# The front of a hybrid decoder layer: attention tiles set into the feature blocks of the input projection, with a ring of three banks

## What is computed

```python
xn = rmsnorm(x, n1)
h, cg, bg, q, k, v, r, a_lr, u, vv, ga, gb, gc = split_cols(xn @ w_in)
conv = sum(cp[:, i:i + t] * conv_w[i] for i in range(3))     # cp = past rows, then cg * h
y_a = (bg * conv) @ proj_a
log_a = log_sigmoid(a_lr @ gla_a2 + gla_a_b) / 16
# gated linear attention, 4 heads (dk 128, dv 256), chunks of 64 tokens
b = cumsum(log_a)                                            # within the chunk
att = where(mask, (q * exp(b)) @ (k * exp(-b)).T, 0)
o_i = att @ v_i + (q * exp(b)) @ s
s = exp(b_last) * s + (k * exp(b_last - b)).T @ v_i
o = rmsnorm(o, gla_ng) * silu(r);  y_b = o @ proj_b
# chunk mixing: chunks of 128 tokens, 4 groups
s = tril(ws) @ rmsnorm(gelu(vv), cm_ng) + bias;  y_c = (gelu(u) * s) @ proj_c
x = x + (sigmoid(ga) * y_a + sigmoid(gb) * y_b + sigmoid(gc) * y_c) @ w_out
x = x + hier_moe(rmsnorm(x, n2));  y = rmsnorm(x, final_g)
```

## Time and profile before

| | us |
|---|---|
| three runs | 2210.21, 2214.68, 2214.86 |
| median | 2214.68 |
| the profiled execution | 2213.19 |
| its span, from the first to the last instruction | 2211.5 |
| TensorE busy in the span | 1819.8 (82%) |
| VectorE, ScalarE, GpSimd busy | 552.6, 458.0, 187.4 |
| bytes moved by DMA | 419 MB, 190 GB/s on average |

### The profile page before, as it was taken

How to read it: one execution, slowest core, us unless ns; L and a number is a source line. 1 busy time by engine, 2 the same in 40 slices (tenths; PEclk the granted TensorE clock), 3 DMA queues, 4 the chain that set the end, 5 groups by cost and what they waited for, 6 DMA issues and landing times. The chain is left out here.

```text
span 2211.5 us, 24670 instructions
## 1 busy us (share of the span) xinstructions
PE 1819.8 (82%) x10166; PEld 1437.6 (65%) x10166; DVE 552.6 (25%) x733; ACT 458.0 (21%) x728; POOL 187.4 (8%) x214
## 2 busy tenths in 40 slices
PE   6999999999999999747765899799329787888770
PEld 6999999999999999624333899688313232333220
DVE  4100100003232200055554543332511001001006
ACT  5122211112211211143443200122001100100112
POOL 0000000000000000111110000000041111111100
PEclk9999999999999999866567999899669999999995
DMA  4222222322366552233313534443659999999976
GB/s 148 98 79 79 94 93 89 133 78 79 113 174 162 130 91 58 103 100 122 122 42 126 206 119 161 143 169 143 279 185 391 421 421 421 421 420 419 417 295 242
DMA packets 176373, 419.37 MB, mean 190 GB/s; under 512 B 38256, under 2 KB 116784, under 8 KB 150624
## 3 DMA queue, kind: packets, MB, share of 16 engines
q1 hardware_dynamic: 153056, 349.00, 44.2%
q0 software_dynamic: 23088, 69.14, 8.2%
q10 hardware_dynamic: 144, 0.03, 0.0%
HBM read 347.53 MB, written 86.33 MB: 196 GB/s over the span
## 5 line engine op out<-in xcount | busy, mean ns | idle before, releaser
L1939 PE MATMUL ps<-W,XT 128*64 128x512 f32 x512 | 257.9, 663 | 83.3 <-DMA W<-in_exp_w_dram 82.0
L1696 PE MATMUL ps<-XH,WH 128*128 128x384 f32 (+1 forms) x1176 | 263.4, 332 | 11.7 <-issue 7.8
L1696 PE MATMUL ps<-XL,WH 128*128 128x384 f32 (+1 forms) x1176 | 260.7, 330 | 0.0
L1696 PE MATMUL ps<-XH,WL 128*128 128x384 f32 (+1 forms) x1176 | 260.2, 329 | 0.0
L1940 PE MATMUL ps<-W,XT 128*64 128x512 f32 x512 | 258.4, 663 | 0.0
L1215 DVE TENSOR_TENSOR WL<-RAW,WH 128x2048 fp32r<-128x2048 f32 x34 | 77.9, 2293 | 631.9 <-ACT WH L928 610.7
L1939 PEld LDWEIGHTS ps<-W,XT 128*64 128x64 f32 x512 | 75.0, 152 | 231.2 <-issue 228.9
L1696 PEld LDWEIGHTS ps<-XH,WH 128*128 128x128 f32 x1176 | 201.4, 189 | 17.3 <-issue 13.5
L1659 PE MATMUL ps<-WH,XH 128*128 128x256 f32 x720 | 206.7, 287 | 5.2 <-ACT OT L936 2.0
L1660 PE MATMUL ps<-WL,XH 128*128 128x256 f32 x720 | 205.2, 285 | 0.0
L1661 PE MATMUL ps<-WH,XL 128*128 128x256 f32 x720 | 205.1, 285 | 0.0
(11 more groups left out here) (284 smaller groups left out, 2320.4 us busy)
## 6 DMA issues: line engine op xcount, KB each, us to landing
W<-in_exp_w_dram SPq DMA_DIRECT2D x192, 1024.0 KB, 25.2
RAW<-in_w_in_dram SPq DMA_DIRECT2D x34, 1024.0 KB, 5.3
feat<-OF POOLq DMA_DIRECT2D x24, 1088.0 KB, 4.4
sg<-feat SPq DMA_DIRECT2D x24, 544.0 KB, 5.5
tokd<-OT POOLq DMA_DIRECT2D x10, 1024.0 KB, 4.7
cbuf<-feat SPq DMA_DIRECT2D x16, 544.0 KB, 5.6
X<-in_x_prompt_dram SPq DMA_DIRECT2D x16, 512.0 KB, 4.4
W<-y SPq DMA_DIRECT2D x8, 1024.0 KB, 7.6
```

Of the source, the lines that this page charges most:

```text
L1696: last = pe.matmul(ps[:, 3 * f + g, 0:tn], w[:, k, :], x[:, k, t0:t0 + tn], start=(k == 0 and i == 0), stop=(k == nk - 1 and i == 2))
L1939: pe.matmul(ps[0:BR, 2 + s, :], XT[s][:, k, 0:BR], pair_of(u, k, DE), start=(k == 0), stop=(k == KD - 1))
```

## The change

The front and the attention stage become one stage; all else stays, but for the barriers' numbers and the places of two buffers. The token chunks are 512 columns wide: five of them (`T_COLS`), vv first, whose nine tiles stay in SBUF (vvt), 24 products with 512 columns for a tile. The sample tile takes the last 128 tokens in place of 64 and padding. The features are blocks of 128 columns, 49 `JOBS` in an order worked out in Python: low-rank, q and k of head 0, the four u, and then one block for each attention step J from -2 to 36, in which the conv features, the gates and the q and k of the next head stand; three gates are left at the end. A block's 72 products are three runs of 24 (`f_product`), one for each token group. All products of the front, the decay's (D), the mixing's (M) and the sample update's (SU) take banks 0 to 2 in turn (`RING`); before a bank is taken the emptying of the one three places before is waited for (`bank_free`, `EMPTIED`), on ScalarE, or on VectorE for cg, bg, M and SU. The attention has bank 3 for its output, bank 4 for both transposes, 5 and 6 for the updates, 7 for the scores.

In block n with step J, TensorE makes the key transpose of tile J + 2 and the scores of J + 1, the first run, the update of J + 1, the second run, the output of J and the transposes of J - 1, the third run, and what `extras` adds. h, cg, bg, u, q and k are no longer stored to DRAM: conv and mixing work on the bank and on SBUF. v and r still go through DRAM and come back tile by tile into five buffers each. The sample states are updated in place, two samples for each bank. The products with the decays are all on VectorE. The squares of vv are ScalarE's, one activation for each tile and group (`v_squares`), 36 in all. The loops of the front are written out.

```diff
+        def front_jobs():
+
+            others = [("H", 0)]
+            for c in range(NCH):
+                if c:
+                    others.append(("H", c))
+                others += [("CG", c), ("G", 3 * c), ("BG", c), ("G", 3 * c + 1), ("G", 3 * c + 2)]
+            others += [("G", g) for g in range(3 * NCH, 3 * KD)]
+            others = iter(others)
+            jobs = [("A", 0, None), ("Q", 0, None), ("K", 0, None)] + [("U", c, None) for c in range(NCH)]
+            for J in range(-2, STEPS + 1):
+                h, j = divmod(J, NT)
+                if 0 <= h < HEADS - 1 and j < 2:
+                    jobs.append(("QK"[j], h + 1, J))
+                else:
+                    jobs.append((*next(others), J))
+            return jobs + [(kind, c, None) for kind, c in others]
+        JOBS = front_jobs()
...
+        def extras(n):
+
+            kind, c, J = JOBS[n]
+            out = []
+            if (kind, c) == ("Q", 0):
+                out += [("D", 0, g) for g in range(3)]
+            if kind == "K" and c:
+                out += [("D", c, g) for g in range(3)]
+            if kind == "U":
+                out += [("M", c, g) for g in range(3)]
+            if J is not None and J > 0 and J % NT == 0:
+                out += [("SU", J // NT - 1, i) for i in range(DEC_B // 2)]
+            return out
...
+        def ring_jobs():
+            out = []
+            for i in range(len(T_COLS)):
+                for t in range(NT):
+                    out.append(("T", i, t))
+                    if (i, t) == (1, 0):
+                        out += [("WS", 0, 0), ("WS", 1, 0)]
+            for n, (kind, c, J) in enumerate(JOBS):
+                out += [(kind, c, g) for g in range(3)] + extras(n)
+            return out
+        RING = ring_jobs()
+        AT = {name: r for r, name in enumerate(RING)}
+        ON_DVE = ("CG", "BG", "M", "SU")
+        EMPTIED, n_of = [], [0, 0]
+        for name in RING:
+            e = int(name[0] in ON_DVE)
+            n_of[e] += 1
+            EMPTIED.append((e, n_of[e]))
...
+            def v_squares(t):
+                if t % 4 == 0:
+                    act.drain()
+                for g in range(NCH):
+                    act.activation(OFA[:, (t % 4 * NCH + g) * P:(t % 4 * NCH + g + 1) * P], vvt[:, t, g * P:(g + 1) * P], ACT.Square, accum_out=vss[:, t * NCH + g:t * NCH + g + 1])
...
+            tw_high(1)
+            t_empty(0, NT - 1)
+            for t in range(NT):
+                v_squares(t)
+            act.drain()
             act.activation(vrs[:], vss[:], ACT.Sqrt, bias=epsc[:], scale=1.0 / P).then_inc(cm_rt, 1)
...
+            for i in range(1, len(T_COLS)):
+                for t in range(NT):
+                    if t == 4 and 1 < i + 1 < len(T_COLS):
+                        tw_high(i + 1)
+                    t_empty(i, t)
...
+            def fw_high(n):
+                act.wait_ge(fw_in[n % 3], n // 3 * 16 + 16)
+                if n >= 2:
+                    act.wait_ge(ring_mm, job_done(n - 2))
+                act.activation(FHI[n % 2][:], FRAW[n % 3], ACT.Copy).then_inc(fw_hi, 1)
...
+            fw_high(0)
+            for n, (kind, c, J) in enumerate(JOBS):
+                if n + 1 < NJ:
+                    fw_high(n + 1)
+                if J is not None and is_tile(J + 2):
+                    k_copy(J + 2)
+                f_empty(kind, c, 0)
+                f_empty(kind, c, 1)
+                if is_tile(J):
+                    out_rms(J)
+                if J is not None and is_tile(J - 1):
+                    out_copy(J - 1)
+                f_empty(kind, c, 2)
+                if n in PREP:
+                    for g in range(3):
+                        decay_logits(PREP[n], g)
+                    decay_log(PREP[n])
+                if n - 2 in PREP:
+                    decay_exp(PREP[n - 2])
+            barrier(act, 1)
...
+            fw_low(0)
+            dve.wait_ge(g_c, 1)
+            for n, (kind, c, J) in enumerate(JOBS):
+                if n + 1 < NJ:
+                    fw_low(n + 1)
+                if J is not None and is_tile(J + 1):
+                    mask(J + 1)
+                if is_tile(J) and J % NT == 0:
+                    sample_queries(J // NT)
+                if is_tile(J) and J % NT == NFULL - 1:
+                    sample_keys(J // NT)
+                f_empty(kind, c, 0)
+                if J is not None and is_tile(J + 1) and (J + 1) % NT < NFULL:
+                    states(J + 1)
+                f_empty(kind, c, 1)
+                if is_tile(J):
+                    out_norm(J)
+                f_empty(kind, c, 2)
+                for what, h, i in extras(n):
+                    if what == "M":
+                        mix_empty(h, i)
+                    if what == "SU":
+                        sample_states(h, i)
+                if n - 1 in PREP:
+                    decay_sums(PREP[n - 1])
+                if n - 3 in PREP:
+                    decayed(PREP[n - 3])
...
+            def bank_free(*name):
+
+                r = AT[name]
+                if r >= 3:
+                    e, count = EMPTIED[r - 3]
+                    pe.wait_ge(ev[e], count)
+                return r % 3
 
...
-            def t_product(all_, tile):
-
-                s = all_.s
-                if not (all_.first and s * NT + tile < 3):
-                    pe.wait_ge(t_ev, all_.n * NT + tile - 2)
-                cols = slice(tile * P, tile * P + P)
+            def t_product(i, t):
+                s, b, cols = i % 2, bank_free("T", i, t), xcols(t)
                 for k in range(KD):
-                    last = three(ps[:, tile % 3, 0:CW], XH[:, k, cols], XL[:, k, cols], WH[s][:, k, :], WL[s][:, k, :],
-                                 k == 0, k == KD - 1)
-                last.then_inc(t_mm, 1)
-
-            def t_chunk(col, st, all_, here):
-                pe.wait_ge(wl_ready, all_.n + 1)
-                for tile in range(NT):
-                    t_product(all_, tile)
-                pe.drain().then_inc(w_used, 1)
+                    if t == 0 and k % 2 == 0:
+                        pe.wait_ge(tw_lo, 4 * i + k // 2 + 1)
+                    last = three(ps[:, b, :], XH[:, k, cols], XL[:, k, cols], THI[s][:, k, :], TLO[s][:, k, :], k == 0, k == KD - 1)
+                last.then_inc(ring_mm, 1)
...
+            def f_product(n, g):
+                kind, c, _ = JOBS[n]
+                b, to, tn = bank_free(kind, c, g), cols_of(g), TG[g][1]
+                if g == 0:
+                    pe.wait_ge(fw_lo, n + 1)
+                for k in range(KD):
+                    hi, lo = FHI[n % 2][:, k, :], FLO[n % 3][:, k, :]
+                    pe.matmul(ps[:, b, 0:tn], hi, XH[:, k, to], start=(k == 0), stop=False)
+                    pe.matmul(ps[:, b, 0:tn], hi, XL[:, k, to], start=False, stop=False)
+                    last = pe.matmul(ps[:, b, 0:tn], lo, XH[:, k, to], start=False, stop=(k == KD - 1))
+                last.then_inc(ring_mm, 1)
...
+            for n, (kind, c, J) in enumerate(JOBS):
+                if J is not None and is_tile(J + 2):
+                    k_transpose(J + 2)
+                if J is not None and is_tile(J + 1):
+                    scores(J + 1)
+                f_product(n, 0)
+                if J is not None and is_tile(J + 1) and (J + 1) % NT < NFULL:
+                    update(J + 1)
+                f_product(n, 1)
+                if is_tile(J):
+                    out_product(J)
+                if J is not None and is_tile(J - 1):
+                    out_transpose(J - 1)
+                f_product(n, 2)
+                for what, h, i in extras(n):
+                    if what == "D":
+                        decay_product(h, i)
+                    elif what == "M":
+                        mix_product(h, i)
+                    else:
+                        sample_update(h, i)
+            barrier(pe, 1)
...
-            def f_chunk(col, st, all_, here):
-                s = st.s
-                pe.wait_ge(wl_ready, all_.n + 1)
-                for f in range(2):
-                    if here.first and here.s == 0:
-                        pe.wait_ge(t_ev, NTC * NT)
-                    else:
-                        pe.wait_ge(f_ev, here.n * 2 + (f - 1))
-                    last = feature(f, WH[s][:, :, f * P:(f + 1) * P], WL[s][:, :, f * P:(f + 1) * P], KD, XH, XL)
-                    last.then_inc(f_mm, 1)
-                pe.drain().then_inc(w_used, 1)
```

More of the change, by code:

```diff
@@ L466, in tok, with bank, head_tile, is_tile @@
+        def bank(*name):
+            return AT[name] % 3
+        def head_tile(J):
+            return J // NT, J % NT
+        def is_tile(J):
+            return J is not None and 0 <= J < STEPS
+        def xcols(t):
+            return slice(t * P, t * P + P) if t < NFULL else slice(NTOK - P, NTOK)
+        def trows(t):
+            return slice(0, P) if t < NFULL else slice(P - NDEC, P)
+        def cols_of(g):
```

(11 more changed lines are left out.)

1253 lines of the change are left out of this document (595 added, 658 removed).

## The result

The kernel after the change takes 2037.8 us (median; 2036.3 to 2038.8) where the one before takes 2214.8: a ratio of 0.9205, 95% interval 0.9189 to 0.9221. The forecast was 2057 with a range of 2036 to 2106, so the sign and the size were right and the sum was 19 us too high. The profiled execution took 2036.3 us, its span 2034.6.

A forecast was written before the change was run, and what follows sets the result against it. TensorE's single queue was taken to bound both stages: feature part starting at 296.9, features 588.0, attention work making 1037.1 us, plus 6 to the first load; with 1011.6 us of unchanged stages, the forecast was 2057 us (2036 to 2106).

The forecast's parts named there:

- first product: Start of the front: longer split of the first weights puts TensorE's first product at 22 us (21 to 25).
- squares' stall: Second token chunk's start: 36 squares on ScalarE delay the emptying; TensorE idles 10.3 us, 13.8 with clock and small groups.
- a full tile: Attention tile set into dense front products: three breaks of 0.09 us, 2.9 us a tile (2.55 to 3.4).
- state update of a head: Attention: four groups of two without waiting for VectorE at each, 4.5 us a head and 0.3 for the ring.
- decay products of a head: Attention's decay products: 0.83 us each, 12 of them 10 us.
- TensorE's end to the first load: End of the front: last emptying, its store and the barrier take 6 us, as before the change.
- tables' stall: First token chunk: ScalarE's Gelu/Sqrt table loads make a 7.3 us path against a 6.3 us period, costing 2.5 us (0 to 6).
- Same-bank pace: Feature products: 24 in a row into one bank might run faster, 7 us less in all; left out of the sum.
- rival 3: Front better than the sum: same-bank pace (7 us), tiles at 2.55 us (11 us), start as now: 2032 us; chance 0.06.
- Rival 1: Front blocks: strictly ordered queues make coupling cost 1.2 us in each of 46 blocks, 2112 us; chance 0.14 beyond 2094.
- Rival 2: Front's ring runs dry: 3.4 us gap plus 2.5 us half clock a time, 2328 us in all 46 blocks; chance 0.06.
- Rival 4: Attention tiles in the front: waiting for vt, rt or sample states, 9.9 us once a head gives 2097 us; chance 0.01.

The follow-up runs named there:

- the kernel with three banks at once: Against the kernel after the change, a feature's three banks filled together, k outermost, with the tile spread over the block: 2225.7 us.
- the row above: Against the kernel after the change, first feature weights split ahead of the token part's last two emptyings, first try: 2036.9 us.
- two banks: Against the kernel after the change, the front's ring has two banks in place of three: 2042.5 us.
- squares later: Against the kernel after the change, squares of vv go four at a time behind the second chunk's emptyings: 2026.4 us.
- both edits: Against the kernel after the change, squares behind the second chunk's emptyings and first feature weights split early: 2020.2 us.
- the repeat of the unaltered kernel: The kernel after the change, unaltered, run again beside the second try of the early split of the first feature weights: 2040.1 us.
- the smaller edit: Against the kernel after the change, first feature weights split ahead of the token part's last two emptyings: 2036.9 us, repeated 2032.0 us.
- the kernel with ten copies: Against the kernel after the change, the high part of each feature's weights made ten times on ScalarE: 2153.4 us.

## Why the prediction was right, and where its sum was off

**What bounds it.** TensorE's queue, added up, gives the time: that step held. The terms against the trace, in us:

| term | forecast | measured |
|---|---|---|
| first product | 22 | 22.84 |
| token part up to the feature part | 272.4 | 266.5 |
| of it: Gelu and Sqrt tables | 2.5 | 0 |
| of it: squares' stall, clock and small groups | 13.8 | 11.1 |
| of it: wait at the feature part's start | 3.1 | 3.1 |
| half clock behind that wait | 2.5 | 1.6 |
| 49 features | 588 | 581.1 |
| a full tile, x 32 | 2.9 | 2.57 |
| a sample tile, x 4 | 5.3 | 5.4 |
| state update of a head, x 4 | 4.75 | 3.8 |
| decay products of a head, x 4 | 2.5 | 2.2 |
| TensorE's end to the first load | 6 | 9.5 |
| first load to the end | 1011.6 | 1016.4 |

**The tables' stall did not happen.** Here a step of the prediction was wrong: a sum over two engines taken as one path, 7.3 us against a period of 6.3 held VectorE's 1.6 us of normalisation, and that runs beside ScalarE's next steps. ScalarE's own cycle, in order of time:

```profile
36.73 0.60 ACT L984 ACTIVATE AR<-ps 128x512 f32<-128x512 f32 x1 [0.84 <-PE ps L1749]
37.23 1.02 ACT L969 ACTIVATE XH<-ps 128x1024 fp32r<-128x1024 f32 x1
38.13 1.06 ACT L962 ACTIVATE OFA<-FW 128x1024 f32<-128x1024 f32 x1
39.08 0.20 ACT L962 ACTIVATION_READ_ACCUMULATOR OFA<-FW 128x1 f32 x1
39.33 1.28 ACT L964 ACT_TABLE_LOAD   x1
40.63 0.29 ACT L964 ACTIVATE rtt<-ssq,epsc 128x1 f32<-128x1 f32 x1
40.94 1.28 ACT L984 ACT_TABLE_LOAD   x1
43.06 0.60 ACT L984 ACTIVATE AR<-ps 128x512 f32<-128x512 f32 x1 [0.84 <-PE ps L1749]
```

It ends 0.84 us before the next bank is full. The two loads of each cycle take 1.28 us apiece, and the root starts 0.02 us behind the first. I quoted the Trainium skill's page "ScalarE: Activation LUTs" in the prediction with 2.7 us for a load; its section "What ACT_TABLE_LOAD costs" has that as the price of a whole switch, 1283 ns for the load and some 1380 ns for a drain. The first figure is the one in these rows. The second does not show in them; with it, by an estimate, the cycle would have been 2.8 us longer and past the period. In the feature part 58 such loads (two for each of 29 steps) cost TensorE nothing.

**The squares were over-priced.** I took 0.37 us for a square and its read; the group has

```profile
L995 ACT ACTIVATE OFA<-AR x36: 292/293/312, 79.9 to 90.5; 128x128 f32<-128x128 f32 x36
L995 ACT ACTIVATION_READ_ACCUMULATOR OFA<-AR x36: 185/186/188, 80.1 to 90.7; 128x1 f32 x36
```

and a pair starts every 0.293 us, since the read of one overlaps the next square: 11.0 us in place of 13.8, which is the 2.7 us by which the gap was shorter. The squares' stall, its place and the engine named in it were as forecast, and taking it away (11.4 us) confirms the cause.

**Same-bank pace.** I kept 12.0 us a feature against my own observation that 24 products into one bank ran 2 ns closer to their columns. It is 11.86; the 7 us that I had left to rival 3 belong to the forecast, and the two kernels with the banks filled in turn, which go back to 0.1667 us, show that it comes from the order of filling. Whether it is the change of bank from product to product or the weights held for three of them, no run separates.

**The tile** at 2.57 us lies at the low end of 2.55 to 3.4. My middle value charged three breaks on top of the steps' spacing in the earlier trace rows, which already held their waits: 11 us too much. The state updates and decay products, which I priced from the stage of before, account for 5 more.

**The end.** From TensorE's end to the first load it takes 3.5 us more than I said. The last store of the front, a gate's 544 KB, is issued by GpSimd at 1009.58 us and has landed 3.0 us later, and the DMAs are idle from 1012 us on (busy share 0.01 and less); but SyncE waits for GpSimd's part of the barrier until 1018.25 us. What GpSimd does in those 5.7 us no row shows. The later stages are 4.8 us longer than in the one profile of the kernel before, within the 5 allowed; 4.4 of it lies in the experts, and only 1.7 of that is TensorE's wait for weights (83.7 against 82.0 us). The change leaves their instructions as they are, and all 13 profiles with the new front are longer there by 3 to 5 us. The cause stays open.

**The rivals.** Rival 1 (1.2 us of coupling a block) is refuted in the kernel as it is: TensorE has no idle time at all between 289.33 and 1008.80 us. But the runs with more ScalarE work show where it begins, and it was not only ScalarE's busy time that decided. Rival 2 came true in the kernel with three banks at once, by a mechanism that I had not named (pieces of tiles that wait for each other). Its half clock of 2.5 us is about right for gaps of over 3 us and too high for nearly all of those of 1 to 2. Rival 3, the better front, came true in two of its three terms, the pace and the tile; the start did not (22.84 us where it had 20.75). Its price was added up wrong: 7, 11 and 1 us from 2057 give 2038, not 2032, and 2038 is what was measured. So the median of 2037.8 lies just inside the range of the forecast, 1.8 us above its lower end, and rival 3 should have had more than 0.06: each of my middle values stood above the fastest row that it came from. Part of the hit is luck, too: the terms that were too high (tables, squares, pace, tile, updates and decays) sum to some 29 us, and the start, the end and the later stages, together 9 us longer than forecast, took some of it back. Without these 9 us the result would have lain below the range. Rival 4 didn't appear: no wait of TensorE names a load in the feature part.

## What to carry to other kernels

A stage that is a chain of small handovers can be hidden in the dense products of another by giving every step a block's distance: here that is worth 93 us. Where in the block the pieces stand is worth nothing as long as the banks are filled one by one, and 156 us where three are filled at once. What can undo it is the order of an in-order queue: ask for each small product which copy it waits for, and what stands ahead of that copy on its engine. When TensorE bounds a sum of many terms, price each from the fastest undisturbed rows, and look for what is not dense (two gaps of 11 us in all here, 15 with the half clock behind them, and 16 to 18 when both were taken away) before more is done to what is.

## What was not expected of the hardware

Engines stop now and then for several microseconds with nothing named. TensorE did inside feature products in four of the other profiles: 3.57 us in the row above, 2.90 us at 602.65 (two banks), 2.18 us at 588.35 (squares later) and 3.00 us at 676.94 (both edits). In the repeat of the unaltered kernel it was ScalarE:

```profile
484.15 0.49 ACT L1062 ACTIVATE OFA<-ps 128x384 f32<-128x384 f32 x1 [7.45 <-remote]
...
487.09 0.30 PE L1828 MATMUL ps<-ident,AR 128*128 128x128 f32 x1 [1.85 <-ACT AR L1106]
```

The bank was full at about 480.3 us, so ScalarE began nearly 4 us late, and the ring let 1.85 us of it through to TensorE, whose products then started 0.32 us apart for 3 us. Its first load is at 1022.29 us, 4.0 later than in the other profile of the same kernel. So one such stop is worth 2 to 5 us, as much as the smaller edit here. In two of these five kernels (two banks, both edits) the profiled execution is also the slowest of all, by 3 to 5 us, so part of the spread between executions may come from such stops. What causes them wasn't found: no run was made for it. Load on the DMAs alone is not it: in the 5 us with the stop their busy share is above 1.0 in two of the five profiles (both edits, and this one) and 0.3 or less in the other three.

The half clock did not follow every gap of 1.3 to 1.9 us. Most in the kernel with ten copies were followed by the full-clock pace, while the 1.85 us just shown, like the 1.93 us there, were followed by the half clock, which came about 1 us after the gap; behind the stop of 2.18 us it did not come at all. What tells these apart stays open.
